# A mixture-of-experts step: gate and up weights loaded and multiplied matrix by matrix instead of by halves of the contraction

## The reference

```python
xt = rms_norm(x, norm_g).reshape(n * t, D_MODEL)          # 520 x 1024
# top 1 of 4 groups, then top 2 of 8 experts in it: comb[t, g, e]
for g in range(N_GROUPS):
    h1 = einsum('td,edf->tef', xt, exp_w1[g])             # gate: 1024 -> 256
    h3 = einsum('td,edf->tef', xt, exp_w3[g])             # up:   1024 -> 256
    act = silu(h1) * h3 * comb[:, g, :, None]
    out = out + einsum('tef,efd->td', act, exp_w2[g])     # down: 256 -> 1024
```

## Time and profile before

| | us |
|---|---|
| runs (three) | 714.54, 716.51, 716.88 |
| median | 716.51 |
| profiled execution, its own time | 719.13 |
| its span, first to last instruction | 717.2 |

### The profile page before, as it was taken

How to read it: one execution, slowest core, us unless ns; L and a number is a source line. 1 busy time by engine, 2 the same in 40 slices (tenths; PEclk the granted TensorE clock), 3 DMA queues, 4 the chain that set the end, 5 groups by cost and what they waited for, 6 DMA issues and landing times.

```text
span 717.2 us, 11659 instructions
## 1 busy us (share of the span) xinstructions
PE 621.9 (87%) x4673; PEld 452.3 (63%) x4673; DVE 319.2 (44%) x629; ACT 201.2 (28%) x343; POOL 78.9 (11%) x129
## 2 busy tenths in 40 slices
PE   4999999989899999999989995999999979489720
PEld 4999998579899999984778872333333333134200
DVE  4748978958544364768413156121121111012038
ACT  6512332254743434435003051121121111012022
POOL 0000000510001210000202111111212111110100
PEclk9999999999999999999989985999999999689965
DMA  9841220323556233679996485999999999999653
GB/s 291 270 140 65 95 82 2 121 79 122 170 129 212 83 118 119 235 236 314 288 387 250 171 309 205 380 412 413 412 416 413 411 414 378 406 411 405 263 239 135
DMA packets 84141, 179.39 MB, mean 250 GB/s; under 512 B 10190, under 2 KB 56970, under 8 KB 78952
## 3 DMA queue, kind: packets, MB, share of 16 engines
q1 hardware_dynamic: 75116, 163.48, 62.1%
q0 software_dynamic: 5600, 12.76, 4.8%
q10 hardware_dynamic: 3372, 2.42, 1.0%
HBM read 172.80 MB, written 15.61 MB: 263 GB/s over the span
## 4 chain that ended last, share of the span: by engine, by line
PE 68%; DMA 9%; SPq 8%; DVE 7%; issue 4%; ACT 3%; ACTq 1%; DVEq 0%; POOLq 0%
PE ps L1684 12%; PE ps L1686 12%; PE ps L1685 12%; PE ps L2128 10%; PE ps L2158 6%; DMA w<-exp_w 6%; SPq L610 5%; PE ps L1833 3%; PE ps L1680 3%; SPq L620 2%; PE ps L1914 2%; DMA raw<-cache_mem_k 2%; PE ps L2014 1%; DMA xs_rows<-x_sample 1%; PE ps L1851 1%
## 5 line engine op out<-in xcount | busy, mean ns | idle before, releaser
L1684 PE MATMUL ps<-xH,w_h 128*128 128x260 f32 x480 | 139.1, 290 | 0.4 <-DVE xL L1342 0.2
L1686 PE MATMUL ps<-xL,w_h 128*128 128x260 f32 x480 | 136.1, 284 | 0.0
L1685 PE MATMUL ps<-xH,w_l 128*128 128x260 f32 x480 | 136.0, 283 | 0.0
L2128 PE MATMUL ps<-w,xeT 128*64 128x512 f32 (+2 forms) x512 | 122.4, 649 | 15.7 <-DMA w<-exp_w 14.3
L2128 PEld LDWEIGHTS ps<-w,xeT 128*64 128x64 f32 (+2 forms) x512 | 40.8, 146 | 95.2 <-issue 91.3
L1684 PEld LDWEIGHTS ps<-xH,w_h 128*128 128x128 f32 x480 | 91.0, 190 | 5.5 <-issue 4.8
L1685 PEld LDWEIGHTS ps<-xH,w_l 128*128 128x128 f32 x480 | 91.0, 190 | 0.3 <-issue 0.2
L1686 PEld LDWEIGHTS ps<-xL,w_h 128*128 128x128 f32 x480 | 91.0, 190 | 0.0
L1034 DVE TENSOR_TENSOR w_l<-raw,w_h 128x2048 fp32r<-128x2048 f32 x28 | 64.1, 2289 | 35.3 <-ACT w_h L731 35.3
L2158 PE MATMUL ps<-w,aT 128*64 128x512 f32 (+2 forms) x256 | 62.0, 635 | 13.8 <-DVE aT L1597 7.6
L731 ACT ACTIVATE w_h<-raw 128x2048 fp32r<-128x2048 f32 x28 | 53.4, 1906 | 25.6 <-PE ps L1686 16.2
(11 more groups left out here) (364 smaller groups left out, 922.1 us busy)
## 6 DMA issues: line engine op xcount, KB each, us to landing
w<-exp_w SPq DMA_DIRECT2D x128, 512.0 KB, 14.8
w<-exp_w SPq DMA_DIRECT2D x32, 1024.0 KB, 19.5
raw<-w_in SPq DMA_DIRECT2D x8, 1024.0 KB, 11.0
raw<-cache_mem_k SPq DMA_DIRECT2D x8, 1024.0 KB, 7.2
raw<-cache_mem_v SPq DMA_DIRECT2D x8, 1024.0 KB, 12.6
raw<-xa_wk SPq DMA_DIRECT2D x4, 1024.0 KB, 5.9
raw<-xa_wv SPq DMA_DIRECT2D x4, 1024.0 KB, 5.6
raw<-xa_wq SPq DMA_DIRECT2D x4, 1024.0 KB, 5.2
```

Source lines behind the costliest of these rows:

```text
L1684: pe.matmul(out, h1, h2, start=start, stop=False)
L1685: pe.matmul(out, l1, h2, start=False, stop=False)
L1686: return pe.matmul(out, h1, l2, start=False, stop=stop)
L2128: last = pe.matmul(mm[0][half, j, :], xeT[j][:, k, half], w13[s][:, :, k, :], start=k == 0, stop=k == KT_D - 1)
```

## The change

Each expert's gate and up weights are no longer split at contraction index 4, but by matrix: `load_half` issues one transfer, the whole gate matrix (h = 0) or the whole up matrix (h = 1), 1 MB with 8 KB per partition, so each semaphore rises by 16 and not by 32. `hidden` makes eight steps with the 256 gate columns into `mm[0][:, j, 0:256]`, then eight with the 256 up columns into the bank `ta[1]`. The end of the gate steps is told by `gate_ready` (`half_ready` before); SP refills the gate regions after it, and ACT's `silu_of` waits for it instead of `hid_ready`. DVE's `gate_of` also waits for `hid_ready` and reads the up product from `ta[1]`.

```diff
             def load_half(s, e, h):
                 dst = w13[s][:].rearrange("p w k f -> p w (k f)")
-                c = slice(h * HALF, h * HALF + HALF)
-                for n, src in enumerate((w1, w3)):
-                    sp.dma_start(dst[:, n:n + 1, c],
-                                 src[bass.ds(e, 1)].rearrange("o p f -> p o f")[:, :, c]).then_inc(w13_in[h][s], 16)
+                src = (w1, w3)[h]
+                sp.dma_start(dst[:, h:h + 1, :], src[bass.ds(e, 1)].rearrange("o p f -> p o f")).then_inc(w13_in[h][s], 16)
...
-                    for h, free in enumerate((half_ready, hid_ready)):
+                    for h, free in enumerate((gate_ready, hid_ready)):
...
             def silu_of(q, j, rs, old=True):
-                act.wait_ge(hid_ready, q + 1)
+                act.wait_ge(gate_ready, q + 1)
...
             def gate_of(q, j, rs, old=True):
                 dve.wait_ge(silu_ready, q + 1)
+                dve.wait_ge(hid_ready, q + 1)
                 if old:
                     dve.wait_ge(at_done, q)
-                dve.scalar_tensor_tensor(gated[:], mm[0][:, j, FF:2 * FF], rs, silu[:], ALU.mult, ALU.mult).then_inc(gated_ready, 1)
+                dve.scalar_tensor_tensor(gated[:], ta[1][:, 0:FF], rs, silu[:], ALU.mult, ALU.mult).then_inc(gated_ready, 1)
...
                 cap = P // len(loads)
-                for k in range(KT_D):
-                    if k % (KT_D // 2) == 0:
-                        for s, count in loads:
-                            pe.wait_ge(w13_in[2 * k // KT_D][s], count * 32)
-                    for n, (s, _) in enumerate(loads):
-                        half = slice(n * cap, (n + 1) * cap)
-                        last = pe.matmul(mm[0][half, j, :], xeT[j][:, k, half], w13[s][:, :, k, :], start=k == 0,
-                                         stop=k == KT_D - 1)
-                    if k == KT_D // 2 - 1:
-                        last.then_inc(half_ready, 1)
-                last.then_inc(hid_ready, 1)
+                for h, ready in enumerate((gate_ready, hid_ready)):
+                    for s, count in loads:
+                        pe.wait_ge(w13_in[h][s], count * 16)
+                    for k in range(KT_D):
+                        for n, (s, _) in enumerate(loads):
+                            half = slice(n * cap, (n + 1) * cap)
+                            last = pe.matmul((mm[0][half, j, 0:FF], ta[1][half, 0:FF])[h], xeT[j][:, k, half], w13[s][:, h, k, :],
+                                             start=k == 0, stop=k == KT_D - 1)
+                    last.then_inc(ready, 1)
```

More of the change, by code:

```diff
@@ L69 @@
 assert COLS <= LIST
-HALF = KT_D // 2 * FF
 RING = 7
@@ L467, in trunk_kernel @@
         hid_ready = sem("hid_ready")
-        half_ready = sem("half_ready")
+        gate_ready = sem("gate_ready")
         silu_ready = sem("silu_ready")
```

## The result

| | before | after |
|---|---|---|
| median of the runs (four each) | 716.69 us | 709.46 us (707.03 to 711.2) |
| ratio, 95% interval | | 0.9903 [0.9875, 0.993] |
| profiled execution, its span | 719.13, 717.2 | 711.2, 709.4 |

The change makes the kernel 7.2 us faster by the medians; repeated beside the experiments it gave 709.4 against 715.2 us, ratio 0.9912 [0.9889, 0.9936]. The forecast was 712.2 us in a range of 708.5 to 716.0: sign and range held, and the gain is some 1.5 to 3 us larger than forecast. The kernel before scatters between 711.5 and 721.2 us in one set of 29 runs, so a single execution tells nothing within 5 us, and the gap between forecast and result is itself not much larger than what the medians can carry.

The account below looks back on a forecast made before the run. The DMA queue from 445 us on, plus what follows the last landing, was taken as the bound. Terms -3.8 (DMA), -0.5 (activation) and +0.03 (PE) gave -4.3 us: 716.51 to 712.2 us, range 708.5 to 716.0.

Parts of the forecast that it names:

- What bounds the kernel: Expert stage: the DMA queue's time from 445 us on, plus what follows the last landing, sets the end.
- The DMA part, -3.8 us: Gate and up loads: 8 KB runs raise 408 to 420 GB/s over 54.5 MB; -3.8 us, bounds -0.9 to -5.2.
- the slow stretch: From 600 to 612 us only half loads pass, at 374 GB/s; against 408 that loses 1.0 us.
- What was priced and left out of the sum: DMA queue: 52 fewer completion writes, 0 to -0.5 us, and the 600 to 612 us stretch, 1.0 us; in the range only.
- Rival (b): DMA queue: more than the rate improves, including completions and the slowest engine; -7.2 us, 709.3 us, chance 0.12.
- Rival (a): DMA queue: packet size hardly matters, engines are limited in bytes; -0.9 - 0.5, about 715.1 us, chance 0.16.
- Rival (c): Hidden products: 64-column tiles can't load side by side, PE becomes the bound; some 740 us, chance 0.06 together with Rival (d).
- Rival (d): POOL's gathers and scatters are held up behind 8 KB packets; 718.7 us, chance 0.06 together with Rival (c).
- The activation, -0.51 us: Last round: silu runs while PE makes the up half, so `gated` starts sooner; -0.51 us, nothing in ordinary rounds.
- the last down weights landed in time and come earlier by the same amount: Last round: down weights, in time for 680.45 us, were assumed to shift earlier equally and so not delay the end.
- The last half at the lower clock: Last hidden half: starts after the same PE pause, so stays at 1.2 GHz and 5.37 us in both kernels.
- The signs: Profile checks: 415 GB/s or more from 447 us, last half near 669, hidden products 6.9 us, early rounds 12.7 us.

Follow-up runs that it names:

- e1: Kernel after, but each gate or up matrix again in two 512 KB transfers with 4 KB runs: 715.02 us, ratio 0.9991 to the kernel before.
- f3: Kernel after with gathers and scatters bounded at 0, so nearly no token rows move: 688.24 us, ratio 0.9619 to the kernel before.
- g3: Kernel after plus twenty idle PE products of 128 columns during the router wait, before the first round: 710.52 us, ratio 0.9921 to the kernel before.
- e2: Kernel after, still one 1 MB transfer per matrix, but laid out in 4 KB runs: 713.78 us, ratio 0.9958 to the kernel before.
- f0: Kernel after, unaltered, measured again beside the experiments: 709.4 against 715.2 us, ratio 0.9912 to the kernel before.
- e4: Kernel before plus six 512-column PE products between the halves of the last hidden products: 718.74 us, ratio 1.0027 to the kernel before.
- g1: Kernel after with 2 KB runs and eight 256 KB gate and up transfers per expert instead of two: 723.29 us, ratio 1.0099 to the kernel before.
- f1: Kernel after, still one 1 MB transfer per matrix, but laid out in 2 KB runs: 721.17 us, ratio 1.0073 to the kernel before.
- g2: Kernel after with token rows spread over other partitions, same rows and bytes: 704.76 us, ratio 0.9847 to the kernel before.
- e3: Kernel after, but silu waits for the end of the up products as before the change: 710.17 us, ratio 0.9913 to the kernel before.
- h1: Kernel before with token rows spread over other partitions: 708.6 us, ratio 0.9903 to the kernel before.

## Why the prediction held, point by point

- **What bounds the kernel**: right. With the transfers as before the gain was gone (e1), without token rows PE became the bound (f3); with the first round 0.9 us shorter no gain was seen (g3), which alone would be too little.
- **The DMA part, -3.8 us**: right in mechanism, and in size as far as can be told. The run length alone is worth 3.3 to 3.9 us by the ratios of e2 and the kernel after, give or take 2.5. That figure holds the slow stretch (388 GB/s in e2, 422 in f0, 1.0 us), which the forecast priced apart; without it some 2.3 to 2.9 us are left, inside the forecast's bounds of 0.9 to 5.2. The choice of 408 against 420 GB/s is what the profiles show (408 to 411, and 418 to 420).
- **What was priced and left out of the sum**: this is the term that was mis-sized. The slow stretch was priced at 1.0 us; 374 became 417 GB/s, 1.3 us in the profiled pair, but the kernel e4, the same as before up to its last round, had 391 there, which leaves 0.8. The completions were priced at 0 to 0.5; the number of transfers measures 0.6 (g1) to 2.4 us (e1, e2). Both belonged in the sum. With them it would have been -5.8, where -5.8 and -7.2 were measured; since the measured price of the runs already holds the slow stretch, that agreement is in part luck.
- **Rival (b)** gave 709.3 and the median is 709.46. Two of its terms came true, but the third, that the slowest engine gains most from larger packets, did not: the slowest engine's last down landing came 6.3 us sooner and the fastest one's 13.8, so that the spread grew from 13.9 to 21.4 us. That the number fits doesn't make it the cause.
- **Rival (a)**, that the queue doesn't care, fell with f1: 2 KB runs cost 11.5 us more than 8 KB.
- **Rival (c)**: no sign of it. A round's hidden products take 6.91 us, as forecast:

```profile
462.69 6.91 PE ps L2126 x64
...
475.44 6.91 PE ps L2126 x64
...
488.20 6.91 PE ps L2126 x64
```

  That is 6.91 / 32 = 216 ns for a step, and rounds are 12.75 us apart. The 64-column tiles of a pair load side by side.
- **Rival (d)**: after the first round's own gather PE waited for none; the chain through the early rounds holds PE and short steps of DVE. In its direction it was nearer the truth than its chance says: token rows and weights do share the engines unevenly, only not so that gathers come late, but so that one engine's weights do.
- **The activation, -0.51 us**: the local saving is there (`gated` 0.10 us after the last product; 0.05 was forecast), its effect on the end is not. It was put on the path because the step "the last down weights landed in time and come earlier by the same amount" was taken over without a look at how the landing spreads. That step failed: they came 6.3 us earlier (678.7 to 672.4) while the rest of the round came 8.3 us earlier (`aT` ready at 672.12 instead of 680.39), and became the last wait.
- **The last half at the lower clock**: failed. The pause did not stay the same; it went from 2.73 to 1.46 us and the clock stayed at 1.00. In the profiled pair this is 1.7 us. Since e1, with the old transfers, shows the full clock there too, it belongs more to that execution of the kernel before than to the change; the medians of the kernel after don't rest on it.
- **The signs**: the rate from 447 us to the last gate or up landing is 413 GB/s where 415 and more was asked; the last half starts at 666.85 where 669 was; a hidden step, the early pace and PE's waits are as foretold. The queue stays fed although SP waits three times as long.

What stays open: how much of the 1.4 us between 447 and 466 us (374 against 404 GB/s) belongs to the change. The profiles fall into order by run length there, 401 to 411 GB/s at 8 KB (f0, g2, after, e3, g3), 363 to 399 at 4 KB (e4, before, e2, h1, e1) and 341 and 357 at 2 KB (f1, g1), so a part does; but those at 4 KB lie 36 GB/s apart among themselves, and the kernel before is at their lower end. Open too is what the number of transfers is worth, 0.6 to 2.4 us by these runs, and why the engines' spread grows with the run length.

## What to carry to other kernels

Where a full DMA queue sets the end, count contiguous runs for each engine, not transfers: a run had a fixed price here (8 to 10 ns), even at 8 KB, so give each partition one long run and leave the number of transfers to what the waits need. Then look how far apart the 16 engines finish the last transfer: if some are done long before the others, uneven small traffic (gathered rows) can be worth as much as the shape of the large transfers (here 1.0% for each, 1.5% together), and changing which partitions hold the rows cost nothing in the rounds. And a saving behind the last landing counts only if the transfer after it has landed as well.

## What the runs showed of the hardware

- With gate and up transfers of 64 partitions, 8 KB each, the queue moved 239 GB/s with the engines booked in full, against 420 with 128 partitions; a packet took 469 instead of 278 ns.
- Run lengths of 8, 4 and 2 KB in the gate and up weights, with the down weights at 8 KB throughout, gave 420, 410 and 393 GB/s in a full queue (f0, e2, f1), and 9.2 ns for each run more by the times.
- Gathers and scatters of 8.5 MB beside 82 MB of weights spread the engines' last completion over 21.4 us (5.0 without them); placing the same rows on every fourth partition made it 10.6 and the kernel 0.6% faster, and the kernel before the change 1.0%.
- After pauses of 1.46 (the kernel after) and 2.31 us (f1) PE's next half took 3.67 us, at 2.4 GHz (granted 1.00 in both); after 2.73 us, in one profiled execution of the kernel before, it took 5.37, with a granted clock of 0.59 at its start, that is 1.2 GHz.
